# A gated recurrence and attention block on one core: the order of loads, transposes and roundings ahead of its first products

## The reference, cut to what matters

```python
mod = silu(c) @ w_ada + b_ada                     # w_ada: 1024 x 3072
shift, scale, gate = split(mod, 3)
h = rms_norm(x, g_pre) * (1 + scale) + shift
proj = h @ w_in                                   # 1024 x 6144, ten column groups
# recurrence over chunks (HGRN2) on four of the groups, differential attention on four
# others, two merge gates; then two branch products, an output product and a residual
```

## Time and profile before

| | us |
|---|---|
| median of three runs | 894.74 |
| lowest, highest | 894.17, 896.36 |
| the profiled execution's own time | 894.62 |
| its span, first to last instruction | 892.6 |
| TensorE busy (matmuls), share of the span | 844.1, 95% |
| VectorE busy | 609.6, 68% |
| ScalarE busy | 471.4, 53% |
| GpSimd busy | 483.2, 54% |
| mean granted TensorE clock | 0.987 of full |

### The profile page before, as it was taken

The page is one execution under the profiler, slowest core; times in us unless marked ns, Lnnn a source line. Parts: engine busy times, 40 slices in busy tenths (PEclk is TensorE's granted clock), DMA queues, the critical chain, the costliest instruction groups (busy, mean ns, idle before and its releaser), DMA issues. The chain is left out here.

```text
span 892.6 us, 13086 instructions
## 1 busy us (share of the span) xinstructions
PE 844.1 (95%) x4781; PEld 664.3 (74%) x4781; DVE 609.6 (68%) x711; ACT 471.4 (53%) x861; POOL 483.2 (54%) x363
## 2 busy tenths in 40 slices
PE   2799899999999999999999999999999999997997
PEld 2677778777777777777777777778788888886885
DVE  3888984788694888684896957856301365768775
ACT  7676323786444875435955437745454641324443
POOL 6054575455455446554545554566778712238884
PEclk9899899999999999999999999999999999999999
DMA  9914131102101111110120121021212561202222
GB/s 330 335 28 162 48 95 48 48 1 72 49 28 45 48 31 41 49 59 13 48 72 2 48 71 48 1 72 48 71 47 69 192 200 50 91 12 95 95 94 95
DMA packets 75586, 68.11 MB, mean 76 GB/s; under 512 B 3652, under 2 KB 65156, under 8 KB 75524
## 3 DMA queue, kind: packets, MB, share of 16 engines
q1 hardware_dynamic: 75408, 67.25, 23.4%
q10 hardware_dynamic: 116, 0.03, 0.0%
HBM read 58.88 MB, written 8.39 MB: 75 GB/s over the span
## 5 line engine op out<-in xcount | busy, mean ns | idle before, releaser
L618 POOL TENSOR_TENSOR w_lo<-w_raw,w_hi 128x512 fp32r<-128x512 f32 x140 | 193.3, 1382 | 256.8 <-ACT w_hi L1190 255.4
L928 PE MATMUL pj<-b_hi,w_hi 128*128 128x512 f32 x728 | 306.7, 421 | 9.7 <-issue 3.6
L930 PE MATMUL pj<-b_hi,w_lo 128*128 128x512 f32 x728 | 286.7, 394 | 0.0
L929 PE MATMUL pj<-b_lo,w_hi 128*128 128x512 f32 x728 | 285.9, 393 | 0.0
L928 PEld LDWEIGHTS pj<-b_hi,w_hi 128*128 128x128 f32 x728 | 137.9, 189 | 53.3 <-issue 14.1
L930 PEld LDWEIGHTS pj<-b_hi,w_lo 128*128 128x128 f32 x728 | 137.5, 189 | 30.7
L929 PEld LDWEIGHTS pj<-b_lo,w_hi 128*128 128x128 f32 x728 | 138.2, 190 | 26.6 <-issue 3.1
L1190 ACT ACTIVATE w_hi<-w_raw 128x512 fp32r<-128x512 f32 x132 | 82.8, 627 | 63.6 <-PE pj L930 57.5
L599 POOL TENSOR_TENSOR w_raw<-w_raw,w_raw 128x512 f32<-128x512 f32 x66 | 92.7, 1405 | 3.7 <-DMA w_raw<-in_w_in 0.8
L679 POOL TENSOR_TENSOR wb_lo<-wb_raw,wb_hi 128x512 fp32r<-128x512 f32 x16 | 23.2, 1449 | 62.8 <-ACT wb_hi L1260 62.8
L696 POOL TENSOR_TENSOR w_lo<-y_all,w_hi 128x512 fp32r<-128x512 f32 x24 | 39.2, 1649 | 16.7 <-ACT w_hi L1356 16.5
(11 more groups left out here) (281 smaller groups left out, 1619.0 us busy)
## 6 DMA issues: line engine op xcount, KB each, us to landing
w_raw<-in_w_in SPq DMA_DIRECT2D x96, 256.0 KB, 4.0
x_in<-in_x SPq DMA_DIRECT2D x8, 512.0 KB, 7.8
ada<-in_w_ada SPq DMA_DIRECT2D x16, 256.0 KB, 6.7
ada<-in_w_ada SPq DMA_DIRECT2D x8, 512.0 KB, 7.4
ada_g<-in_w_ada SPq DMA_DIRECT2D x8, 512.0 KB, 3.8
res<-in_x SPq DMA_DIRECT2D x8, 512.0 KB, 4.1
out_x<-rows_o SPq DMA_DIRECT2D x7, 512.0 KB, 2.9
o_kepta<-oa SPq DMA_DIRECT2D x4, 512.0 KB, 5.9
```

The lines of the kernel that those rows point to most:

```text
L618: pool.tensor_tensor(w_lo[slot(v)][:, :], raw[:, :], w_hi[slot(v)][:, :].bitcast(F32), ALU.subtract).then_inc(s_wlo, 1)
L928: pe.matmul(bank[:, :], wh, part(b_hi[m], kk), start=(fresh and kk == 0), stop=False, skip_group_check=True)
L929: pe.matmul(bank[:, :], wh, part(b_lo[m], kk), start=False, stop=False, skip_group_check=True)
L930: last = pe.matmul(bank[:, :], wl, part(b_hi[m], kk), start=False, stop=(kk == 3), skip_group_check=True)
```

## The change

1. Loads: the first two weight blocks, x tiles 0 to 3, the first piece of w_ada, the next two weight blocks, the second piece, x tiles 4 to 7, the third piece. Before: x 0 to 3, two weight blocks, x 4 to 7, two weight blocks, the three pieces.
2. TensorE: three matmuls on constants and the first mod columns come before any transpose; only transposes 0 to 3 precede the first products, the other twelve stand among them, six of them in one bank (`XT_BANKS`), each waiting for the eviction of the block that had its bank before. In the second token half, kh=0, the tiles j=0 and 1 are done by kk with a transpose after each step, then the mod columns of piece 3, then j=3, and only then j=2 (the fourth tile ahead of the third). The split of weight block v=6 waits for all four.
3. ScalarE scales x tiles 0 to 3 and 7, VectorE 4 to 6. Blocks 0, 1 and 4 to 7 get shift and scale in the eviction itself (`x_out_affine`), blocks 2, 3 and 8 to 11 from VectorE (`DVE_AFFINE`), 12 to 15 from ScalarE as before. block_high(2) and (3) stand behind the squares of tiles 4 to 7.
4. VectorE's order: three sums of w_ada ahead of the first norm, the second norm behind block_low(3), the third piece's sums between the low parts 4 to 7, the four sums for M5 and M6 spread.
5. Two early roundings by ScalarE: M5's between block_high(11) and (12), M6's ahead of forget(0, 1). VectorE subtracts M5's before the loop. M7's and M4's move from slots 24 and 28 (rounding) to 20 and 24, and from 26 and 30 (subtraction) to 22 and 27.

```diff
-SUM_HIGH_AT = {16: M6, 20: M5, 24: M7, 28: M4}
-SUM_LOW_AT = {17: M6, 21: M5, 26: M7, 30: M4}
+SUM_HIGH_AT = {20: M7, 24: M4}
+SUM_LOW_AT = {17: M6, 22: M7, 27: M4}
...
-        XT_BANKS = [0, 1, 2, 3, 4, 5, 6, 0, 4, 5, 6, 4, 5, 6, 4, 5]
+        XT_BANKS = [4, 5, 6, 3, 4, 5, 4, 5, 4, 5, 6, 6, 6, 6, 6, 6]
...
+            load_half(0, 0)
+            for t in range(4):
+                load_x(t)
+            for kk in range(KT):
+                load_ada(0, kk)
+            load_half(1, 0)
+            for kk in range(KT):
+                load_ada(1, kk)
+            for t in range(4, NT):
+                load_x(t)
+            sp_.wait_ge(s_acc, KT)
+            for kk in range(KT):
+                load_ada(2, kk)
...
-            for n in range(KT):
-                x_block(n)
             pe.wait_ge(s_const, N_CONST)
+            pe.wait_ge(s_acc, 2)
+            for _ in range(3):
+                pe.matmul(first_banks[0][0], ident[:, :], sc[:, 0:HALF], start=True, stop=True)
             pe.wait_ge(s_vec, 1)
             mod_columns(0)
-            pe.wait_ge(s_xt, KT)
-            for _ in range(2):
-                pe.matmul(first_banks[3][0], ident[:, :], sc[:, 0:HALF], start=True, stop=True)
+            for n in range(4):
+                x_block(n)
             for kk in range(4):
                 pe.wait_ge(s_bl, kk + 1)
                 for j in range(4):
                     if kk == 0:
                         pe.wait_ge(s_wlo, j + 1)
+                        if j == 2:
+                            x_block(4)
+                            x_block(5)
+                        if j == 3:
+                            pe.wait_ge(s_xt, 4)
                     first_product(j, 0, 0, kk)
                 if kk == 0:
                     mod_columns(1)
-                elif kk < 3:
-                    for n in range(4):
-                        x_block(KT + 4 * (kk - 1) + n)
+                if kk == 2:
+                    x_block(6)
+                    x_block(7)
+            for n in range(KT, KT + 3):
+                x_block(n)
+            for kk in range(4):
+                pe.wait_ge(s_bl, 4 + kk + 1)
+                for j in range(2):
+                    if kk == 0:
+                        pe.wait_ge(s_xt, KT + j + 1)
+                    last = first_product(j, 0, 1, kk)
+                    if kk == 3:
+                        last.then_inc(s_proj, 1)
+                x_block(KT + 3 + kk)
             mod_columns(2)
-            pe.wait_ge(s_xt, 2 * KT)
-            for j in range(4):
+            x_block(2 * KT - 1)
+            for j in (3, 2):
                 if j == 3:
                     pe.wait_ge(s_mod, len(PIECES))
+                else:
+                    pe.wait_ge(s_xt, 2 * KT)
...
+            act.wait_ge(s_rsq, 1)
+            for t in range(4):
+                scale_x(t)
+            for e in range(2):
+                x_out_affine(e)
+                block_high(e)
+            x_out(2)
+            x_out(3)
+            square(4)
+            square(5)
+            x_out(4)
+            x_out(5)
+            square(6)
+            square(7)
+            block_high(2)
+            block_high(3)
             root(1)
             act.wait_ge(s_rsq, 2)
-            for n in range(4):
-                x_out(n)
...
+            scale_x(7)
             x_out(6)
             x_out(7)
...
+            for e in range(4, 8):
+                x_out_affine(e)
+                block_high(e)
             for n in range(KT + 4, 2 * KT):
                 x_out(n)
...
+            for kk in range(4):
+                block_high(8 + kk)
+                affine(12 + kk)
+            act.wait_ge(s_t1, 4)
+            act.activation(b_hi[M5][:, :], b_raw[M5][:, :], ACT.Copy).then_inc(s_bhi[M5], 1)
+            for e in range(12, 16):
+                block_high(e)
...
+            act.wait_ge(s_t2, 4)
+            sum_high(M6, b_raw[M6])
             forget(0, 1)
...
+            for kk in range(3):
+                add_ada(0, kk)
             norm(0)
...
+            for kk in range(3, KT):
                 add_ada(0, kk)
             add_ada(1, 0)
             add_ada(1, 1)
             mod_piece(0)
             add_ada(1, 2)
+            block_low(0)
             add_ada(1, 3)
...
+            mod_piece(1)
+            affine(2)
+            affine(3)
+            block_low(2)
+            block_low(3)
+            norm(1)
             add_ada(2, 0)
+            dve.wait_ge(s_rsq, 2)
+            for t in range(4, NT - 1):
+                scale_x(t)
             add_ada(2, 1)
...
+            for e in range(4, 8):
+                block_low(e)
+                add_ada(2, e - 1)
             add_ada(2, 7)
+            sum_5(0)
+            sum_5(1)
             mod_piece(2)
+            for e in range(8, 12):
+                affine(e)
+            sum_5(2)
             for kk in range(4):
                 block_low(8 + kk)
+                if kk == 0:
+                    sum_5(3)
             for kk in range(4):
                 block_low(12 + kk)
+                sum_6(kk)
...
+            sum_low(M5, b_raw[M5])
```

More of the change, by code:

```diff
@@ L101, in dve_reads @@
     return sum((m % PROD) in ADDED for m in range(2 * PROD, n + 1))
+DVE_AFFINE = [2, 3] + list(range(8, 12))
 SLOTS = 2 * STEPS
@@ L827, in x_block @@
                     pe.wait_ge(s_xnb, 4)
[L828 to L831 removed]
+                taken = [e for e in range(n) if XT_BANKS[e] == XT_BANKS[n]]
+                if taken:
+                    pe.wait_ge(s_xt, taken[-1] + 1)
                 for t in range(4):
@@ L1490, in block_low, with sum_low, affine, sum_5 @@
                                   ALU.subtract).then_inc(s_bl, 1)
-            norm(0)
-            dve.wait_ge(s_rsq, 1)
-            for t in range(4):
-                scale_x(t)
-            norm(1)
-            for kk in range(KT):
+            def sum_low(m, raw):
+                dve.wait_ge(s_bhi[m], 1)
+                dve.tensor_tensor(b_lo[m][:, :], raw[:, :], b_hi[m][:, :].bitcast(F32), ALU.subtract).then_inc(s_blo[m], 1)
+            def affine(e):
+                kh, th, kk = e // 8, e // 4 % 2, e % 4
+                t = part(xq[kh][th], kk)
+                dve.wait_ge(s_xt, KT * th + 4 * kh + kk + 1)
+                dve.wait_ge(s_mod, 2 if kh == 0 else 3)
+                dve.tensor_scalar(t, t, mod_s[:, 4 * kh + kk:4 * kh + kk + 1], mod_b[:, 4 * kh + kk:4 * kh + kk + 1],
+                                  ALU.mult, ALU.add).then_inc(s_b, 1)
+            def sum_5(kk):
+                dve.tensor_tensor(part(b_raw[M5], kk), part(xq[0][1], kk), part(xq[0][0], kk), ALU.subtract).then_inc(s_t1, 1)
+            def sum_6(kk):
+                dve.wait_ge(s_t1, kk + 1)
+                dve.wait_ge(s_ba, kk + 1)
+                dve.tensor_tensor(part(b_raw[M6], kk), part(xq[1][1], kk), part(b_raw[M5], kk), ALU.subtract).then_inc(s_t2, 1)
+            for kk in range(3):
+                add_ada(0, kk)
+            norm(0)
+            for kk in range(3, KT):
                 add_ada(0, kk)
```

113 lines of the change are left out of this document (35 added, 78 removed).

## The result

The changed kernel takes 896.89 us (median; 895.93 to 898.48) against 893.99 us of the kernel before on the same chip. The ratio is 1.0027 with a 95% interval of 1.0017 to 1.0037. It is slower by 2.4 us by the ratio and 2.9 by the medians. The forecast was 1 us faster, so the sign is wrong. The time lies outside the forecast's own range (892.0 to 896.0) and inside the wider one (890.0 to 897.4). By the ratio the difference is just inside the bound of telling of 0.3%, 2.7 us, but its interval excludes no change.

A forecast was written before the change was run, and what follows sets the result against it. Bound: TensorE's work before 106 us, its level 3 waiting on VectorE's chain. A 3.6 us lead after M7's sum, less 2.6 for subtractions, left 1.0: 894.6 - 1.0 = 893.6 us, own range 892.0 to 896.0, wider 890.0 to 897.4.

The forecast's parts named there:

- the 2.6 of the forecast: VectorE before level 2's copy: M4's subtraction moved there and M7's perhaps meeting GpSimd cost 2.6 us, between 2.3 and 4.3.
- End of the M7 sum: 73.3 (70.5 to 76.9): VectorE's sum for M7, with 2.8 us of GpSimd collision, ends at 73.3 us; it was 74.3 before.
- First product "24.3": TensorE's first product starts at 24.3 us, 7.5 us earlier than before.
- 33.4: Third contraction block: its rounding and subtraction, behind the squares of x tiles 4 to 7, end at 33.4 us.
- 42.4: Second token half: after transpose 8, affine eviction, rounding and subtraction, TensorE's next product starts at 42.4 us.
- 51.2: VectorE's last sum of w_ada ends at 50.8 us, or 51.2 where GpSimd's weight split overlaps it.
- The last shift and scale at 53.5: After mod columns and two small steps, the last shift and scale comes at 53.5 us, 2.5 us later than before.
- The first of the last eight short operations starts at 61.3: VectorE starts the last four subtractions and four sums for M6 at 61.3 us, after ScalarE's chain including M5's rounding.
- 9.2 and 2.8: VectorE's eight short operations plus M4 and M7 take 9.2 us undisturbed; GpSimd collisions add 2.8, bounds 0 and 6.4.
- at nothing: Terms costed at zero: moved gain scalings, M6's earlier rounding, changed bank list, v=6's wait for four groups, SP's wait.
- M4 before level 2: Slower rival, chance 0.15: a late last shift and scale leaves M4's 3.3 us before level 2 unpaid, giving 898 us.
- a forecast lead of 1.0: At VectorE's level 2 copy, the changed kernel was to be 1.0 us ahead of the kernel before.

The follow-up runs named there:

- after_sums_ahead: Changed kernel with sums 1 to 4 of the third w_ada piece ahead of block_low(4), then one behind each of low parts 4 to 6: 894.33 us.
- after_m5_behind: Changed kernel with M5's rounding by ScalarE behind block_high(15) instead of ahead of block_high(12): 895.08 us.
- before_extra: Kernel before with four extra 128x512 multiplications on VectorE at slot 21, their output unread: 901.38 us.
- before_roundings: Kernel before with part 5 of the change alone (early M5 and M6 roundings, M7 and M4 moved): 893.00 us.
- after_mended: Changed kernel with the four edits of after_x_first, after_sums_ahead, after_sum5_behind and after_m5_behind together: 893.92 us.
- after_x_first: Changed kernel with x tiles 0 to 3 loaded ahead of the first two weight blocks: 895.40 us.
- after_sum5_behind: Changed kernel with VectorE's sum_5(0) and (1) moved from ahead of mod_piece(2) to behind affine steps 8 to 11: 896.22 us.
- mended_mul_late: after_mended with the first head's two gate multiplications and their sigmoids moved from slots 31 and 34 to 43 and 45, behind dq's eviction: 890.71 us.

## Why the prediction was wrong

**What was right.** The bound: TensorE's time up to 106 us decides, and up to the copy of level 2 VectorE's chain holds it; TensorE's lead of 5 to 7 us at first doesn't matter; the third mod piece comes later than before; M5's and M6's subtractions follow M7's sum at once; the wait before level 3 stays as it was (3.01, "3 us") with its slow clock; M4's subtraction stretches to 3.27 beside GpSimd, while M7's did not (2.28). Four subtractions ahead of that copy took 10.0 us where three took 7.9 before: 2.2 more, against the 2.6 of the forecast.

**The step that failed** is "End of the M7 sum: 73.3 (70.5 to 76.9)". It ended at 77.7, past the bound that I had given. The 4.4 us are:

- First product "24.3": 26.46. x tile 0 landed at 8.3, not "near 6". That, and the rounding of the third block (TensorE at kk=2 at 35.19, "33.4"), moved the next product to 44.40 ("42.4"). VectorE's sums of the third piece caught up some of it: the last ended at 52.6, "51.2", 1.4 late. Besides, I had treated the rounds as limited by a steady 1.95 us each, and not seen that VectorE would be idle for 2.63 us just ahead of them, while sums of that piece were still to be done. That is a cost of the change which the forecast carried unseen, not a part of the 4.4; after_sums_ahead shows its price, 1.8 us at M7's sum and 2.6 in the time.
- "The last shift and scale at 53.5": 56.45. Behind the last sum I had counted the mod columns and two small steps, 2.3 us. It was 3.8: sum_5(0) and (1) ran beside GpSimd (2.77 for two that take 1.28 in after_sums_ahead) and ended 0.6 behind the mod columns, and a small step took 1.03 where it took 0.16 before, 0.9 more. That is 1.5 in all.
- "The first of the last eight short operations starts at 61.3": 64.51, another 0.3. M5's rounding in front was counted, at 1.91, and cost 1.8 there (after_m5_behind: the wait fell from 2.33 to 0.54). What I never asked is whether it had to stand there.
- From there to M7's end 12.0 by the forecast (9.2 and 2.8): 13.2, the last 1.2. GpSimd's split of v=6, which I had starting at 59 to 61 while VectorE waits, started at 63.92, as it waits for the fourth group of products; so nearly all of its work ran beside VectorE's short operations, which took 3.9 more than when free, not 2.8. The wait of v=6 for four groups stood among the terms "at nothing", looked at for its weights alone; it ties GpSimd's start to TensorE's kh=1, and so to the late third piece. That it is what made the collision larger is argued from these rows: no run took the wait away.

**The rival "M4 before level 2"** (slower, 0.15, 898) named its condition well: M7's sum at 76.5 or later. It came true, and its sign too. Its mechanism did not hold: with M4 back behind level 2 the time is 897.5. Its work costs the same wherever it stands ahead of dq. I had followed VectorE only to the copy of level 2, that TensorE waits for, and the chain goes on to the eviction of dq. But that is the smaller error: the sum had gone wrong before the copy, which is 2.9 late against a forecast lead of 1.0, and behind it 0.7 were won back.

**The balance.** M7's sum is 3.4 later than before; the vanished wait for M6's rounding gives back 2.6; the fourth subtraction ahead of level 2's copy costs 2.2. 3.4 - 2.6 + 2.2 = 3.0, and the copy is 2.9 later (101.58 against 98.70). TensorE's level 3 hands this on. From the copy to dq VectorE has 3.7 us less to do, mainly because M4's subtraction is gone from there, but it waits 3.48 us for TensorE's level 4 in the slow stretch (0.48 before): 0.7 are won back, and 2.2 are left at dq. So behind level 3 the late link in the changed kernel is TensorE at half clock, and no longer VectorE's own work. Undoing by parts gives the same picture, if parts add up: part 5 alone gains 1.8 to 2.4 on the kernel before; so parts 1 to 4 cost 4 to 5. In the changed kernel the single edits gave 1.5 (loads), 0.7 (sum_5), 2.6 (sums) and 1.8 (M5) by the medians, and 1.7, nothing, 3.3 and 1.3 by the ratios. Parts 2 and 3, the order on TensorE and the moved scalings, were not undone in any run.

**On the two rules of the Trainium skill.** Ports (SBUF — State Buffer, "Who interferes with whom"): the rows agree that a VectorE instruction of two SBUF inputs is held for up to about one GpSimd instruction, 4 x 0.63 becoming 6.86 in before_extra. By it all of GpSimd's work from v=6 to the first sum would collide, and the M7 sum would have been forecast 2.3 later, at 75.6. The rows lie between: 3.9 us of lengthening, against 2.8 forecast and 5.1 by that reading. Clock (TensorE: Matmul & The Clock Gate, "PE-mode transpose"): by it the transposes among products would have cost a slow stretch. Twelve transpose blocks stand between 29.2 and 55.1, and the granted clock was 1.00 from 29.3 to 56.6; this case doesn't show it. The slow stretch at 56.6 came behind mod columns, one transpose block and 1.38 us of waiting, and no run tells these apart. Nor do the rows that I had set against the rule show a change of the clock: the granted clock is 1.00 both where 17 transposes took 3.47 us and where they took 1.92.

**Left open.** Why the clock falls for 10.2 us behind some waits of 3 us for dq (before_roundings, before_extra) and not behind another of 2.96 (after_mended) is not settled; the same kernel's times scatter by 4 us and more with it. Why a wait of about 3 us before level 3 is followed by 6.8, 3.4 or no us at half clock is open too. What the wait of v=6 and parts 2 and 3 cost by themselves was not tried.

## What to carry to other kernels

Follow the engine that a late instruction sits on past the first wait that it causes, until it has idle time again: here that was 40 us and three waits later, and in nine of fourteen profiles the start of one eviction told the end. When moving work to start something earlier, look for idle time just ahead of the bound engine's remaining work (2.6 us here, filled by swapping two sums) before touching loads or the other engines. An early start that brings a chain beside another engine's work can lose part of what it gained: with four edits M7's sum ended 6.1 us earlier than in the changed kernel, dq started 5.0 earlier and the profiled execution ended 4.9 earlier. And take a second profile before you split 1 us: stretches with the same code ended 1.1 and 1.6 us apart here.

## What the runs showed of the hardware

- Four VectorE multiplications of 128x512 took 6.86 us beside GpSimd, 1.72 each, where three subtractions of this size took 1.89; two subtractions of 128x2048 took 4.49 in one order and 6.00 in another. GpSimd's instructions lengthen too: a split's copy of 128x512 took 0.61 us in the changed kernel and 6.27 in after_mended, beside a row of such VectorE operations.
- The first x tile landed at 8.3, 6.5 us after its issue at 1.8; issued first it landed at 4.4. The two weight blocks ahead of it, 512 KB, cost 3.9 us here at the very start, not the 1.5 counted from the earlier trace rows. In the table of stretches the DMA engines moved 162 GB/s from 4 to 6 us at a busy share of 0.90, where the kernel before moved 383 at 1.00.
- Slow stretches of TensorE came as 3.4, 6.8 or 10.2 us at a granted clock of 0.50 (1.2 instead of 2.4 GHz). Behind a wait of 2.98 to 3.04 us before level 3 it was 6.8 us in the kernel before and the changed kernel, 3.4 in four profiles (after_x_first, after_sum5_behind, after_sums_ahead, after_m5_behind) and none in mended_mul_late. Two executions with 10.2 us behind the wait for dq ended 4.1 us later, counted from dq, than the nine.
